# Recurrent mixer, first group: second product directly behind the first, and the first product's copy ahead of the bias additions

## What is computed

```python
def rglru_mixer(u, w_in, b_in, conv_w, conv_b, w_gx, b_gx, w_ga, b_ga, lam, w_out, b_out):
    proj = u @ w_in + b_in                                  # 256 x 2560
    ybr = jax.nn.gelu(proj[..., :LRU_WIDTH])
    xbr = causal_dwconv(proj[..., LRU_WIDTH:], conv_w, conv_b)
    xh = xbr.reshape(bsz, s, LRU_HEADS, LRU_BLOCK)          # 10 heads of 128
    gx = jax.nn.sigmoid(einsum('bshi,hij->bshj', xh, w_gx) + b_gx)
    ga = jax.nn.sigmoid(einsum('bshi,hij->bshj', xh, w_ga) + b_ga)
    log_a = LRU_C * ga * jax.nn.log_sigmoid(lam)
    a_t = jnp.exp(log_a)
    b_t = jnp.sqrt(-jnp.expm1(2.0 * log_a)) * gx * xbr
    _, h = lax.associative_scan(_linear_combine, (a_t, b_t), axis=1)
    return (h * ybr) @ w_out + b_out
```

## Time and profile before

| | us |
|---|---|
| median of 3 runs | 2386.7 |
| lowest and highest | 2386.51, 2388.38 |
| profiled execution, its time | 2384.55 |
| profiled execution, its span | 2382.9 |
| TensorE busy | 2075.6 |
| VectorE busy | 1161.0 |
| ScalarE busy | 437.8 |

### The profile page before, as it was taken

One profiled execution on the slowest core, in us unless ns is written; L12 is line 12 of the kernel. 1 busy time (PEld: TensorE's weight loads), 2 busy tenths in 40 slices (PEclk: granted clock), 3 DMA queues, 4 the chain that ended last, 5 costly groups with the idle time before them and its releaser, 6 DMA issues. The chain is left out here.

```text
span 2382.9 us, 30126 instructions
## 1 busy us (share of the span) xinstructions
PE 2075.6 (87%) x12452; PEld 1433.4 (60%) x12452; DVE 1161.0 (49%) x2277; ACT 437.8 (18%) x906; POOL 51.0 (2%) x65
## 2 busy tenths in 40 slices
PE   7999999997666666666666699999999999999998
PEld 5787888862222222222221258878999459899953
DVE  6999897331000001101110028564877656687774
ACT  2232211220000000000000012351333014333311
POOL 0111110000000000000000000000000000000000
PEclk9999999998877878787787799999999999999999
DMA  8758876789999999999999996443554446544530
GB/s 297 262 122 251 230 203 226 263 372 428 427 428 428 428 429 428 428 429 428 429 428 427 428 407 224 161 155 120 175 177 159 178 146 237 205 166 162 177 141 18
DMA packets 161037, 668.95 MB, mean 281 GB/s; under 512 B 11237, under 2 KB 64014, under 8 KB 131998
## 3 DMA queue, kind: packets, MB, share of 16 engines
q1 hardware_dynamic: 148638, 645.15, 68.7%
q0 software_dynamic: 11008, 16.78, 3.6%
q10 hardware_dynamic: 1280, 5.44, 0.6%
HBM read 666.27 MB, written 17.86 MB: 287 GB/s over the span
## 5 line engine op out<-in xcount | busy, mean ns | idle before, releaser
L1776 PE MATMUL PS<-arena,hT 128*32 128x512 f32 x2048 | 307.4, 742 | 160.5 <-DMA arena<-in_w_up_dram 125.8
L1776 PEld LDWEIGHTS PS<-arena,hT 128*32 128x32 f32 x2048 | 65.3, 125 | 381.1 <-DMA arena<-in_w_up_dram 200.3
L1830 PE MATMUL PS<-arena,hT 128*32 128x512 f32 x1008 | 171.0, 815 | 92.3 <-DMA arena<-in_w_down_dram 86.4
L1413 PE MATMUL PS<-hT,arena 128*128 128x256 f32 (+1 forms) x1136 | 247.8, 380 | 0.6 <-ACT hT L845 0.6
L2313 DVE SCALAR_TENSOR_TENSOR arena<-arena 128x512 f32<-128x512 f32 (+2 forms) x514 | 246.3, 546 | 0.8
L2316 DVE TENSOR_TENSOR arena<-arena 128x1024 f32<-128x1024 f32 (+2 forms) x283 | 232.1, 841 | 27.4 <-PE PS L2112 23.1
L2316 DVE TENSOR_TENSOR hT<-hT,PS 128x512 f32<-128x512 f32 x16 | 16.4, 1027 | 463.9 <-PE PS L1776 463.9
L1413 PEld LDWEIGHTS PS<-hT,arena 128*128 128x128 f32 (+1 forms) x1136 | 210.9, 189 | 32.6 <-issue 2.8
L2068 PE MATMUL PS<-hT,arena 128*128 128x128 f32 x1408 | 164.9, 275 | 0.6 <-DVE hT L2316 0.6
L2068 PEld LDWEIGHTS PS<-hT,arena 128*128 128x128 f32 x1408 | 160.9, 192 | 1.0 <-DVE hT L2316 1.0
L1830 PEld LDWEIGHTS PS<-arena,hT 128*32 128x32 f32 x1008 | 32.8, 130 | 213.8 <-DMA arena<-in_w_down_dram 136.4
(11 more groups left out here) (347 smaller groups left out, 2434.4 us busy)
## 6 DMA issues: line engine op xcount, KB each, us to landing
arena<-in_w_gate_dram SPq DMA_DIRECT2D x64, 2048.0 KB, 40.9
arena<-in_w_up_dram SPq DMA_DIRECT2D x64, 2048.0 KB, 40.7
arena<-in_w_down_dram SPq DMA_DIRECT2D x63, 2048.0 KB, 38.3
arena<-in_ffn_w_up_dram SPq DMA_DIRECT2D x32, 2048.0 KB, 8.2
arena<-in_w_in_dram SPq DMA_DIRECT2D x36, 1024.0 KB, 8.7
arena<-in_ffn_w_down_dram SPq DMA_DIRECT2D x16, 2048.0 KB, 7.8
arena<-in_w_ada_dram SPq DMA_DIRECT2D x12, 2048.0 KB, 12.4
arena<-in_ssd_w_in_dram SPq DMA_DIRECT2D x10, 2048.0 KB, 9.9
```

Source lines behind the costliest of these rows:

```text
L1413: mm = pe.matmul(dsts[i % parts], l, r, start=(i < parts), stop=(i >= parts * (n - 1)), skip_group_check=parts > 1)
L1776: mm = pe.matmul(PS[32 * f:32 * f + 32, 1 + half, :], xe[:, 32 * (2 * pi + k):32 * (2 * pi + k) + 32], w[:, k, 512 * f:512 * f + 512], sta ...
L1830: mm = pe.matmul(PS[32 * q:32 * q + 32, 4 + n, :], htr[:, P * q + 32 * pi:P * q + 32 * pi + 32], w[:, q, 512 * n:512 * n + 512], start=(pi ...
```

## The change

On ScalarE the copy of the first product (`l_p1(0)`) is issued ahead of the four bias additions instead of behind the first of them, and the copy `l_u2(0)` behind all four instead of behind the third. On TensorE the second product of group 0 (`l_second(0)`) is issued directly behind the first product and ahead of S1T1, instead of behind S2T2. The other groups keep their order. No instruction is added or taken away, and no wait value changes.

```diff
@@ -1238,14 +1238,12 @@
+            l_p1(0)
             for t in range(4):
                 act.wait_ge(s["raw_ev"], 4 * PRE.index("mix_pre1") + t + 1)
                 act.activation(pads[:, t, 3:3 + T], pads[:, t, 3:3 + T], ACT.Identity, bias=l_bias(t)
                                ).then_inc(s["ly_ready"], 1)
-                if t == 0:
-                    l_p1(0)
-                if t == 2:
-                    l_u2(0)
+            l_u2(0)
             l_u3(0)
@@ -2256,11 +2254,14 @@
                 if n < L_GROUPS - 1:
+                    if n == 0:
+                        l_second(n)
                     l_s1t1(n)
                     if n:
                         lru_gates((0, 6)[n - 1])
                     l_s2t2(n)
-                    l_second(n)
+                    if n:
+                        l_second(n)
```

## The result

The changed kernel takes 2388.01 us against 2385.73 (medians of 22 runs each, 2.3 us apart). The ratio of the two kernels over all these runs is **1.0013, with a 95% interval of 1.0008 to 1.0019**, or +3.1 us with +1.9 to +4.5 us. It is slower, by less than the 0.2% that the prediction called no change.

A forecast was written before the change was run, and what follows sets the result against it. TensorE, busy for 87% of the span, was taken to bound the kernel, through what starts its run in group 0. Terms -1.72 + 2.36 + 1.02 = +1.66 us took the median 2386.7 to 2388.4 us, range 2386.0 to 2391.2.

The forecast's parts named there:

- the sum: Group 0 up to S3T3's weight loads: -1.72 + 2.36 + 1.02 = +1.66 us, ends 1.59 and 1.73, passed on whole.
- the forecast: Whole kernel: 2388.4 us, longer by 1.66 us at full clock; chance 0.52.
- rival A: TensorE's clock falls after the longer stall before the second product, costing 1.70 us more: 2390.1 us; chance 0.34.
- Part 1: ScalarE's first product copy ahead of the bias additions: S2T2 no longer waits for it, -1.72 us.
- Part 2: Second product directly behind the first on TensorE: waits for VectorE's first scaling, stalling everything behind it, +2.36 us.
- Part 3: S3T3 directly behind S2T2: nothing hides its wait for ScalarE's copy of S2T2's result, +1.02 us.
- Part 4: Other bias additions, VectorE's queue, the group's last product and the loads it releases: no added cost.
- The wait before S3T3: TensorE's second idle time, of 1 us, which may take up part of the loss from a fallen clock.
- against: Argument against the clock falling: stall no longer than the only case; the 1 us idle before S3T3 may absorb part.
- B: Bank 4 already free, so the second product fills TensorE's stall: -1.3 us, 2385.4 us; chance 0.03.
- C: TensorE's clock stays low, at once or in two falls: over 0.2% slower, about 2391.5 us or more; chance 0.05.
- D: Hidden slack in some wait between 1978.7 and 2014.4 absorbs part of 1.66 us: 2386.7 to 2388; chance 0.06.

The follow-up runs named there:

- e1_copy_first: Kernel before with only ScalarE's half: first product's copy ahead of the bias additions, TensorE's order unchanged; ratio 0.9998 (0.9989 to 1.0007).
- e3_kept_busy: Changed kernel plus six matmuls of ones, result never read, in TensorE's stall before the second product; ratio 1.0005 (0.9996 to 1.0014).
- e5_tile0_scaled_first: Changed kernel with VectorE scaling raw tile 0 ahead of its operand sums; 8.55 us from first product's load to S3T3's, changed kernel 12.95.
- e4_between: Changed kernel with the second product one place later, behind S1T1; 9.48 us from first product's load to S3T3's, changed kernel 12.95.
- a3_changed_again: Changed kernel profiled again, nothing altered; 11.32 us from first product's load to S3T3's, against 12.95 in its first profile.
- e3_kept_busy_again: Second profile of the changed kernel with six matmuls of ones in the stall; 11.27 us from first product's load to S3T3's, changed kernel 12.95.

## Why the prediction was right, and where it was not

- *Direction and range.* 2388.4 us was forecast and 2388.0 measured, inside the range. The difference between the kernels is another matter: it is +3.1 us by the ratio, and the sum's 1.66 lies below its interval of 1.9 to 4.5. The median's closeness is partly luck: the median of before came out 1 us lower with more runs, which hid most of what the sum lacks. What the ratio agrees with is the forecast and rival A mixed: 1.71 + 0.6 x 1.62 = 2.7 us, if the clock falls in three of five executions. A fall in every execution would give 3.35, which fits as well; how often it falls over many executions is not known.
- *Part 1, the copy, -1.72 us.* Right at S3T3: `e1_copy_first` has M lower by exactly 1.72. The remark that the half by itself "is a gain of the whole stall" holds only up to there; VectorE's 22 part takes 1.1 of it back (W lower by 0.60). The expectation of `e1_copy_first` has this, the prediction has not. It made no difference to the sum, since with the change TensorE is late and not early.
- *Part 2, the stall, +2.36 us.* The second product was put at 4.89 us behind the first load; it came at 4.92 (4.86 in `e3_kept_busy`). `e5_tile0_scaled_first` shows that the scaling of tile 0 is the whole reason.
- *Part 3, the lost cover, +1.02 us.* 1.06 in `e4_between`.
- *Part 4, the rest at nothing.* Right: the shift at S, W and near 2014 us is the shift at M, within 0.05 us (at M, S and W 3.35, 3.35 and 3.33 in the changed kernel; 1.72, 1.71 and 1.70 in `a3_changed_again`).
- *The sum* was 1.66 with ends 1.59 and 1.73; measured 1.72 and 1.73 where the clock stays, 1.66 and 1.67 with the stall filled.
- *Rival A* had the right mechanism and nearly the right price (1.70; 1.62 measured at M). The wait before S3T3 took up none of it: it is 0.97 us between the loads in all six executions, because it follows the copy of S2T2 and moves with it. Its **chance** was too low: 0.34 against 0.52 for the forecast, while it came in three of five executions. The step that failed is the "against": a stall 0.07 us shorter than the one case in the trace (2.80 against 2.87) was taken to be less likely to lower the clock than not. One case tells that a stall of this size can do it; it gave no ground for a chance below one half. The same stall of the first block, read in all 14 profiles, lowered the clock in twelve.
- *Rivals B, C and D* did not come. No execution had a second fall.

## What to carry to other kernels

A product that is moved up to fill a wait brings its own wait along, and everything queued behind it pays for that: look up when its output bank comes free, on the engine that frees it, before moving it. A product that stands between two steps of a chain through another engine is cover; moving it away costs the round trip less one product, here 1.06 us. And price a new stall on TensorE twice, once for its length and once for the clock afterwards.

## What was not expected of the hardware

The clock after one and the same stall (2.80 to 2.81 us by the matmuls and 2.96 to 2.97 by the loads, in all six executions) fell in four executions and stayed in two, and a fall cost the same 1.62 us at M each time. Behind group 0's stalls of up to 1.65 us between loads, before the change and in the other variants, it never fell in these profiles.

The two executions in which it stayed are also the only two of 14 in which it stayed behind the stall of the first block. Of the twelve falls there, eleven lost 1.70 to 1.72 us of clock, and that of `e3_kept_busy_again` lost 2 x (0.09 + 3 x 0.50 + 0.12) = 3.42 us, twice as much, behind a stall of 2.88 us. So the price of a fall, too, was not the same everywhere.
